# Gate products moved from ScalarE and GpSimd to VectorE, and the window bias stored in whole runs of 16 queries

## The reference, cut to what matters

```
h      = rmsnorm(x) * g_mix
p      = h @ w_in                      # queries, keys, values, conv input, latents, gate logits
window = softmax(q k^T / 8 + bias[head, distance], sinks) v     # 8 heads, keys of this block of 128 and the one before
latent = causal attention over a compressed key/value (ckv) and one shared rotary key (kpe)
conv   = 31-tap depthwise convolution, normalised
x      = x + (sum over 3 branches of sigmoid(gate logits) * (branch @ w_branch)) @ w_out
```

## Time and profile before

| | |
|---|---|
| median of 3 runs | 4863.44 us (4861.99 to 4865.29) |
| the profiled execution | 4864.94 us, span 4863.1 us |
| busy, share of the span | PE 84%, PEld 69%, DVE 46%, ACT 30%, POOL 3% |
| the opening | from 0 to 52.9 us; PE starts the projection at 63.04 us |
| window and latent attention of layer 1 | about 157 to 466 us |
| the same of layer 2 | about 1116 to 1424 us |

### The profile page before, as it was taken

How to read it: one execution, slowest core, us unless ns; L and a number is a source line. 1 busy time by engine, 2 the same in 40 slices (tenths; PEclk the granted TensorE clock), 3 DMA queues, 4 the chain that set the end, 5 groups by cost and what they waited for, 6 DMA issues and landing times. The chain is left out here.

```text
span 4863.1 us, 70463 instructions
## 1 busy us (share of the span) xinstructions
PE 4100.0 (84%) x29198; PEld 3345.2 (69%) x29198; DVE 2234.5 (46%) x3547; ACT 1453.8 (30%) x2611; POOL 124.8 (3%) x97
## 2 busy tenths in 40 slices
PE   6888999988889999699948888799997656657998
PEld 5666777766667777567737777688886545545887
DVE  4575544436755443334564444433333444354434
ACT  3334432223344222324222222322223201433322
POOL 0111000001100000000000000000000000000000
PEclk8999999999989999879969999899998766777999
DMA  4331444423314443100100000121121001001322
GB/s 155 89 93 50 132 156 157 160 75 95 79 56 152 156 158 137 44 14 1 61 4 3 4 3 22 38 67 61 61 68 47 6 0 35 18 0 61 96 95 78
DMA packets 320251, 338.93 MB, mean 70 GB/s; under 512 B 25792, under 2 KB 298848, under 8 KB 313696
## 3 DMA queue, kind: packets, MB, share of 16 engines
q1 hardware_dynamic: 315520, 330.56, 21.2%
q10 hardware_dynamic: 4448, 4.36, 0.3%
HBM read 313.92 MB, written 20.97 MB: 69 GB/s over the span
## 5 line engine op out<-in xcount | busy, mean ns | idle before, releaser
L276 DVE TENSOR_TENSOR weights_lo<-weight_ring,weights_hi 128x1024 fp32r<-128x1024 f32 x370 | 453.4, 1225 | 1410.0 <-ACT weights_hi L272 1410.0
L272 ACT ACTIVATE weights_hi<-weight_ring 128x1024 fp32r<-128x1024 f32 x370 | 392.2, 1060 | 1633.0 <-PE banks L323 1554.3
L323 PE MATMUL banks<-mlp_x_lo,weights_hi 128*128 128x512 f32 (+1 forms) x1280 | 480.3, 375 | 0.0
L323 PE MATMUL banks<-mlp_hidden_hi,weights_hi 128*128 128x512 f32 (+1 forms) x1280 | 477.1, 373 | 0.0
L323 PE MATMUL banks<-mlp_hidden_lo,weights_hi 128*128 128x512 f32 (+1 forms) x1280 | 476.6, 372 | 0.0
L323 PE MATMUL banks<-mlp_hidden_hi,weights_lo 128*128 128x512 f32 (+1 forms) x1280 | 476.0, 372 | 0.0
L2568 PE MATMUL banks<-weight_ring 64*64 64x64 f32 x10368 | 341.2, 221 | 86.4 <-DVE weight_ring L2686 45.7
L2568 PEld LDWEIGHTS banks<-weight_ring 64*64 64x64 f32 x10368 | 320.5, 137 | 105.2 <-DVE weight_ring L2686 52.9
L323 PE MATMUL banks<-mlp_x_hi,weights_hi 128*128 128x512 f32 x768 | 308.1, 401 | 20.2 <-DVE mlp_x_lo L307 9.5
L323 PE MATMUL banks<-mlp_x_hi,weights_lo 128*128 128x512 f32 x768 | 305.4, 398 | 0.0
L323 PEld LDWEIGHTS banks<-mlp_hidden_hi,weights_hi 128*128 128x128 f32 x1280 | 240.8, 188 | 52.6 <-issue 6.7
(11 more groups left out here) (533 smaller groups left out, 7361.3 us busy)
## 6 DMA issues: line engine op xcount, KB each, us to landing
weight_ring<-in_w SPq DMA_DIRECT2D x64, 1024.0 KB, 5.5
mod_chunks<-in_mod_w SPq DMA_DIRECT2D x24, 2048.0 KB, 10.3
weight_ring<-in_w_in SPq DMA_DIRECT2D x41, 1024.0 KB, 5.2
weight_ring<-in_w_up SPq DMA_DIRECT2D x32, 1024.0 KB, 5.7
weight_ring<-in_w_down SPq DMA_DIRECT2D x32, 1024.0 KB, 5.1
weight_ring<-in_w_in SPq DMA_DIRECT2D x52, 512.0 KB, 3.8
weight_ring<-in_w_out SPq DMA_DIRECT2D x16, 1024.0 KB, 5.3
gate_logits_dram<-gates_staged SPq DMA_DIRECT2D x48, 256.0 KB, 3.5
```

The source lines that it names most:

```text
L272: act.activation(self.w_hi[:, t % 2], self._raw(t), ACT.Copy).then_inc(self.w_rounded, 1)
L276: dve.tensor_tensor(self.w_lo[:, t % 2], self._raw(t), self.w_hi[:, t % 2].bitcast(F32), ALU.subtract)\
L323: mm = pe.matmul(bank, a[:, k, :], b[:, k, t0:t0 + w], start=(k == 0 and n == 0), stop=(k == KD - 1 and n == 2))
```

## The change

The opening: no fill and no `masked`. Each table gets rows of 257 values for 16 queries, POOL writes the mask into the values that are not bias, ACT writes the 128 bias values between them, and SP stores the 16 rows of a head as one run of 4112 values. There are three tables in place of eight, so from the fourth group of chunks on ACT waits until the stores that last read the table have landed (`stored`, one semaphore for each table).

The gate tiles: ACT's copy and POOL's product become one DVE instruction that reads PSUM and `row`, behind `rest(n + 2)`. `emptied` now counts finished tiles for PE and for SP's store. POOL's copies of the rotary key come as soon as `placed` is reached.

```diff
@@ opening
-    pieces, chunks, parts_out = 4, 32, len(bias)
+    pieces, chunks, parts_out = 4, 32, 8
+    piece, held, row_out = SEQ * 8, P // parts_out, 2 * P + 1
...
-                sp.wait_ge(filled, 16 * BLOCKS)
                 for n in range(parts_out):
                     sp.wait_ge(taken, (n + 1) * chunks // parts_out)
+                    width = held * row_out if n < parts_out - 1 else (held - 1) * row_out + P + 1
                     for b in range(BLOCKS):
-                        src = bias[n][32 * b:32 * b + 8].rearrange("h (q k) -> h q k", k=P)
-                        sp.dma_start(rows_of(b, P // parts_out * n, P // parts_out), src).then_inc(stored, 16)
+                        sp.dma_start(rows_of(b, n, width), bias[n % len(bias)][32 * b:32 * b + 8, 0:width])\
+                            .then_inc(stored[n % len(bias)], 16)
...
-                pool.memset(masked[:, :], MASKED).then_inc(blank, 1)
+                for n in range(len(bias)):
+                    pool.memset(table(n)[:, :, 0:1], MASKED)
+                    pool.memset(table(n)[:, :, P + 1:], MASKED).then_inc(blank, 1)
...
-                act.wait_ge(blank, 1)
-                for b in range(BLOCKS):
-                    act.dma_start(bias_dram[b].rearrange("h q k -> q h k"), over(masked[:, :], SWA_HEADS))\
-                        .then_inc(filled, 16)
...
                 for c in range(chunks):
                     act.wait_ge(made, c + 1)
-                    own = chunks // parts_out
-                    act.activation(bias[c // own][:, c % own * BANK:(c % own + 1) * BANK], ps[:, c % 8, :], ACT.Copy)\
-                        .then_inc(taken, 1)
+                    n, at = c // 4, c % 4 * 4
+                    if at == 0 and n < len(bias):
+                        act.wait_ge(blank, n + 1)
+                    elif at == 0:
+                        act.wait_ge(stored[n % len(bias)], stores_of(n - len(bias)))
+                    act.activation(table(n)[:, at:at + 4, 1:P + 1], ps[:, c % 8, :].rearrange("p (q k) -> p q k", k=P),
+                                   ACT.Copy).then_inc(taken, 1)
@@ class Gates
-    def evacuate(self, act, n):
-        act.wait_ge(self.summed, n + 1)
+    def evacuate(self, dve, n):
+        dve.wait_ge(self.summed, n + 1)
         rows, out = self.place(n)
         if n >= 5:
-            act.wait_ge(self.stored[n % 3], 16 * ((n - 2) // 3))
-        act.activation(out, self.banks[n % 2][rows, :], ACT.Copy).then_inc(self.emptied, 1)
+            dve.wait_ge(self.stored[n % 3], 16 * ((n - 2) // 3))
+        dve.tensor_tensor(out, self.banks[n % 2][rows, :], self.row[rows, :], ALU.mult).then_inc(self.emptied, 1)
...
     def act(self, act, halves):
         for n in self.finished(halves):
             self.round(act, n + 2)
-            self.evacuate(act, n)
-
-    def pool(self, pool, halves):
-        for n in self.finished(halves):
-            rows, out = self.place(n)
-            pool.wait_ge(self.emptied, n + 1)
-            pool.tensor_tensor(out, out, self.row[rows, :], ALU.mult).then_inc(self.scaled, 1)
 
     def dve(self, dve, halves):
         for n in self.finished(halves):
             self.rest(dve, n + 2)
+            self.evacuate(dve, n)
@@ window_attention, opening, POOL
             pool.wait_ge(padded, 1)
-            gates.pool(pool, (0, 1))
+            beside.pool(pool)
```

More of the change, by code:

```diff
@@ L822, in opening @@
     nc, ph, ps = kit.nc, kit.ph, kit.ps
-    pieces, chunks, parts_out = 4, 32, len(bias)
-    piece = SEQ * 8
+    pieces, chunks, parts_out = 4, 32, 8
+    piece, held, row_out = SEQ * 8, P // parts_out, 2 * P + 1
     rows = slice(64, P)
@@ L836, in opening @@
         reached = nc.alloc_sbuf_tensor_at("reached", [P, 2, piece], F32R, offset=REACHED_AT)
-        masked = sb("masked", [P, 2 * P])
         angle, turns, sig = sb("angle", [P, SEQ]), sb("turns", [P, SEQ]), sb("c_sigmoid", [P, 16])
-        small_in, consts_in, pos_in, pack_in, x_in, blank, filled = (
-            ph.sem(f"open_{s}") for s in ("small", "consts", "pos", "pack", "x", "blank", "filled"))
+        small_in, consts_in, pos_in, pack_in, x_in, blank = (
+            ph.sem(f"open_{s}") for s in ("small", "consts", "pos", "pack", "x", "blank"))
         stepped, spread_out, cut, compared, made, taken, reduced, bent, rope_done, zeroed = (
@@ L843, in opening, with rows_of, stores_of, table @@
                                           "rope", "zeroed"))
-        def rows_of(b, q0, n):
-            return bass.AP(bias_dram.tensor, bias_dram[b, 0].offset + 1 + q0 * (2 * P + 1),
-                           [[2 * P * P, SWA_HEADS], [2 * P + 1, n], [1, P]])
+        def rows_of(b, n, width):
+            return bass.AP(bias_dram.tensor, bias_dram[b, 0].offset + held * n * row_out,
+                           [[2 * P * P, SWA_HEADS], [1, width]])
+        def stores_of(n):
+            return 16 * BLOCKS * (n // len(bias) + 1)
+        def table(n):
+            return bias[n % len(bias)].rearrange("p (q k) -> p q k", k=row_out)
         with ph as block:
@@ L971, in __init__ @@
         self.landed, self.stored = [sem(f"landed{s}") for s in range(2)], [sem(f"stored{s}") for s in range(3)]
-        self.rounded, self.ready, self.summed, self.emptied, self.scaled = (
-            sem(n) for n in ("rounded", "ready", "summed", "emptied", "scaled"))
+        self.rounded, self.ready, self.summed, self.emptied = (
+            sem(n) for n in ("rounded", "ready", "summed", "emptied"))
         part = 2 * KD * P
@@ L989, in store @@
         if n >= 2:
-            sp.wait_ge(self.scaled, n + 1)
+            sp.wait_ge(self.emptied, n + 1)
             sp.dma_start(self.logits[n - 2], self.staged[:, n % 3, :]).then_inc(self.stored[n % 3], 16)
@@ L1133, in _ @@
                 closing(sp)
[L1135 to L1141, removed]
         @block.tensor
@@ L1266, in __init__ @@
         self.keys, self.gated = keys, gated
-        self.spread, self.timed, self.folded, self.placed, self.copied = (
-            kit.ph.sem(f"kpe_{s}") for s in ("spread", "timed", "folded", "placed", "copied"))
+        self.spread, self.timed, self.folded, self.placed = (
+            kit.ph.sem(f"kpe_{s}") for s in ("spread", "timed", "folded", "placed"))
     def sync(self, sp, u, adjusted):
@@ L1277, in tensor @@
         if u == 1:
-            pe.wait_ge(self.gates.scaled, 2)
+            pe.wait_ge(self.gates.emptied, 2)
             pe.matmul(self.kit.ps[:, 7, :], self.kit.const("mla_spread"), self.kpe, start=True, stop=True)\
@@ L1292, in vector, with pool @@
                 .then_inc(self.timed, 1)
-    def pool(self, pool, done):
-        pool.wait_ge(self.gates.scaled, done)
+    def pool(self, pool):
         pool.wait_ge(self.placed, 1)
         for hd in range(1, MLA_HEADS):
-            ins = pool.tensor_copy(self.keys[64:P, hd, :], self.keys[64:P, 0, :])
-        ins.then_inc(self.copied, 1)
-        pool.wait_ge(self.copied, 1)
+            pool.tensor_copy(self.keys[64:P, hd, :], self.keys[64:P, 0, :])
     def scalar(self, act, u):
@@ L1514, in _ @@
             pool.tensor_scalar(turned, turned, -1.0, None, ALU.mult).then_inc(negated, 1)
-            for halves in plan:
-                gates.pool(pool, halves)
         @block.tensor
@@ L1858, in load_bias @@
                         if b == 0:
-                            sp.wait_ge(*bias_stored)
+                            for sem, count in bias_stored:
+                                sp.wait_ge(sem, count)
                         k = slice(P if b == 0 else 0, 2 * P)
@@ L3579, in second_block @@
         norm(kit, "final_norm", x_lat, KD, SEQ, lambda j, n: cols("final", 1, j), h[:, :, 0:SEQ], store=d["out"])
-BIAS_ROOM = [(113920, 3), (187648, 5)]
+BIAS_ROOM = (113920, 187648, 187648 + 16 * (2 * P + 1) * 4)
 REACHED_AT = 138496
@@ L3610, in build @@
             cos_sin = first.enter_context(nc.sbuf_tensor("rope_cos_sin", [P, SEQ], F32))
-            bias, size = [], SEQ * 8 * 4 // 2
-            for at, count in BIAS_ROOM:
-                bias += [nc.alloc_sbuf_tensor_at(f"bias_by_distance{at + n * size}", [P, size // 4], F32,
-                                                 offset=at + n * size) for n in range(count)]
-            stored, _ = kit.ph.held_sem("bias_stored")
+            bias = [nc.alloc_sbuf_tensor_at(f"bias_by_distance{n}", [P, 16 * (2 * P + 1)], F32, offset=at)
+                    for n, at in enumerate(BIAS_ROOM)]
+            stored = [kit.ph.held_sem(f"bias_stored{n}")[0] for n in range(len(bias))]
             opening(kit, d, x2, pack_sb, cols, cvec, cos_sin, bias_dram, bias, stored)
-            first_block(kit, x, d, bias_dram, (stored, 16 * BLOCKS * len(bias)), logits, cos_sin, pack_sb, cvec, mods)
+            counts = [48 * BLOCKS, 48 * BLOCKS, 32 * BLOCKS]
+            first_block(kit, x, d, bias_dram, list(zip(stored, counts)), logits, cos_sin, pack_sb, cvec, mods)
         second_block(kit, x2[:, :, :], d, pack_sb, cols, [mods[:, 0], mods[:, 1]])
```

## The result

The changed kernel takes 4871.83 us (median of 20 runs, 4864.28 to 4874.23) and the kernel before 4863.2 us (median of 20 runs, 4859.05 to 4867.27). The ratio is 1.0015, 95% interval 1.0009 to 1.0021: 7.3 us slower by it, within the 0.2% that were called no change. The profiled execution has 4872.83 us, span 4871.0, against 4864.94.

What follows compares the result with a forecast made beforehand. SP's bias stores were taken to bound the opening, and DVE mostly the window attention. Opening +14.5 us and attentions -10 us gave +4.5, so 4868 us; range 4840 to 4890, the forecast's own 4855 to 4873.

Steps and rivals of the forecast that it cites:

- two terms of opposite sign: Opening +14.5 us, because the first weights queue behind slower stores; attentions of both layers -10 us, from -4 to -20.
- The chain's start: Opening, DVE's bias chain: without the fill it starts earlier than 8.37 us, 4.5 at the lowest; 2.4 us gained.
- The stores' rate: Opening, SP's bias stores: 4.19 MB in place of 2.1 at 83 GB/s, through at 70.0 us, PE starting at 77.5.
- Rival 2: Opening: stores run in step at 52 GB/s, 4896 us; it decides from about 73 GB/s down, opening costing 20. Chance 0.34.
- ACT's new wait: Opening: ACT waiting for a free table does not starve the stores; the copies end at some 55 us.
- No tap over 0.8 us: Attentions, DVE: expected sign in the changed kernel's profile that no single tap takes longer than 0.8 us.
- step 2's taps: Window attention, DVE: eight taps of 8.92 us become 6.15 with the new product, -2.8 us in a layer.
- Copies of the key: POOL's seven rotary key copies begin about 204 us in DVE's idle time, not beside taps; 2.8 us a layer.
- The tiles on the path: Attentions: -0.35 us per gate tile; four and a half of nine count, -1.5, plus three latent places, -1.0, each layer.
- PE's wait for exponentials: Window attention: PE's 14.9 us of waiting in a layer falls by about 5 us.
- Rival 3: Opening: only 512-byte pieces were slow, stores keep up with copies, PE starts at 46, total 4836 us. Chance 0.20.
- Rival 4: Attentions: DVE's product holds up PE or softmax, or taps get no shorter; +36 us, with the opening 4914. Chance 0.04.

Runs made afterwards that it cites:

- the gates alone: The kernel before with its old opening, but the change's gate tiles (product on DVE, rotary key copies earlier): 4849.37 us, ratio 0.9969.
- before again: The kernel before, unchanged, profiled once more: 4863.61 us.

## Why the prediction was right, and where its terms were not

The total was forecast at 4868 and came out at 4871.8, inside the forecast's own range. The signs and places of the terms were right, but the closeness of the total is luck: two terms of opposite sign were both too small, by 9 us and by 10 or more, and some 4 to 8 us came on top in the second block.

- **The chain's start**: 2.4 us gained as taken, for the wrong reason. The inputs came 4.9 us earlier, and POOL's memsets, which I had put at nothing because ACT did not need the tables before 13 us, took 2.5 back from DVE's casts. I had asked who waits for the memset and not what runs beside it.
- **The stores' rate**: this is the step that failed. 83 GB/s was taken from shorter runs because the rate "looks like a bandwidth that the source has". It was the source, but 83 was read from 512-byte pieces, of which up to eleven were under way at once; with long pieces, at most eight at once, in the queue's order 0, 1, 2, 3 it is 72 (last bytes landed at 78.06 us, forecast 70.0). Rival 2 had the mechanism, and its threshold, "about 73 GB/s", was met: the opening cost the 20 us and more that it named. The weights behind the stores took 8.9 us from the last byte to PE where 7.5 was reckoned. +23.9 in place of +14.5.
- **ACT's new wait**: as forecast, it starves nobody; the copies end at 58.8 us (forecast 55) while the stores queue to 74.
- **No tap over 0.8 us**: right; none of 240 is, where 53 were before. So was the price of step 2's taps, 5.98 for 6.15, and that the product on DVE makes PE wait nowhere.
- **Copies of the key**: -5.6 forecast, 4.7 measured in medians.
- **The tiles on the path**: wrong in both factors. The price of a tile, -0.35, was read from one tile whose taps were held up 1.04 us; over all 52 POOL's product costs DVE 0.71, and with the emptying counted DVE has 0.2 us less a tile. The count was four and a half of nine in the window attention and three places in the latent one, 5 us in two layers; the runs give 11 for the product's move alone, about as much as DVE's busy time falls over all 52. How many tiles lie on the path isn't shown, since the clock has a part in it. The gain of the traces, -20 in both stretches with the gates alone (644.0 to 623.7), is more than DVE's 16.3 us. PE's busy time falls there by 8.6 us, from 551.6 (550.1 in before again) to 543.0, and is 543.2 and 541.8 in the changed kernel's two profiles, with the granted clock at 0.93 to 0.94 in place of 0.92 to 0.93. I had no term for the clock; what raised it isn't shown.
- **PE's wait for exponentials**: 3.0 us less in layer 1, about 5 forecast.
- **Rival 3**, long runs are cheap, was right for another kernel: it needs the heads spread as well, and then gives the early start that it named (48.9, "46").
- **Rival 4** fell: taps got shorter in every kernel without POOL's product.
- **The second block** (+3.6 and +7.8) was in no term.

The fastest version here is the changed kernel with the heads on every fourth partition: 4834.5 us, 0.9936 of before (0.9920 to 0.9953). An eight-of-sixteen limit of DMA engines on its 198 GB/s was not tried, since the halves went as one packet.

## What to carry to other kernels

When a store is slow, ask which partitions it reads before asking how long its runs are: the same bytes went at 72, 106, 132 and 198 GB/s by the choice of partitions and the order of blocks alone, and long runs paid only once the shared way out was free. Ahead of moving an operation to or from POOL, list the DVE instructions that run beside it; here POOL's 1.8 us product cost DVE 0.71 us for each tile on average, as much as the 0.68 of doing it on DVE, and memsets that nobody waits for yet made four tiny copies take 5.8 us. Take such a price over many instances: the one that I read had 1.04. And where two terms of opposite sign nearly cancel, time each alone: the whole looked like no change and was a loss of about 25 us and a gain of about 20.

## What I had not expected of the hardware

- Two limits on one transfer that are near each other (512-byte runs 98 GB/s, shared ports 72) hide each other: from 83 GB/s, lifting one alone gave 98 or 72 (with twice the bytes), lifting both 198.
- The issue order of four DMAs on one queue is worth 34 GB/s (72 to 106), and 18 us of the opening, in the one run that tried it.
- A collision of DVE and POOL costs both: the seven copies of the key took 7.08 us beside the taps and 3.98 alone. POOL's memset of 1.81 us held up a copy of 32x8 elements for its whole length.
- Two descriptors for adjoining halves of a run left SBUF as one packet of 16,448 bytes.
